# v's tiles between and behind the passes read the passes' own x operands, and VectorE takes the mixes out of PSUM

## The reference

```python
D_MODEL = 1024; SEQ = 2048; DEC_BATCH = 8; DEC_SEQ = 16; PAST_LEN = 128
D_A = D_B = 512; N_GROUPS_A = 4; GMLP_CHUNK = 128; N_HEADS_B = 8; CHUNK = 64; LEFT_CHUNKS = 8
D_IN = 3 * D_A + 4 * D_B

def _project(x, w_in, ln_v_g, ln_v_b):
    h = jnp.einsum('bsd,de->bse', x, w_in)
    u_a = gelu(h[0:512]); v_a = _layernorm(gelu(h[512:1024]), ln_v_g, ln_v_b); z_a = h[1024:1536]
    q, k, v_b, z_b = h[1536:2048], h[2048:2560], h[2560:3072], h[3072:3584]

def _sgu_prompt(u, v, w_s, b_s):                 # chunks of 128 frames, 4 groups of 128 channels
    mix = jnp.einsum('gts,bnsgc->bntgc', jnp.tril(w_s), vc) + b_s.T[None, None, :, :, None]
    return u * mix.reshape(b, s, D_A)

def _band_attn_prompt(q, k, v, rel_table):       # own chunk of 64 and 8 before it, 8 heads
    scores = jnp.einsum('bnqhd,bnkhd->bnhqk', qc, kb) * (HEAD_DIM_B ** -0.5) + bias
    o = jnp.einsum('bnhqk,bnkhd->bnqhd', softmax(where(valid, scores, -inf)), vb)

def _merge(x, a_out, z_a, b_out, z_b, w_out, g, bb):
    y = jnp.concatenate([a_out * jax.nn.silu(z_a), b_out * jax.nn.silu(z_b)], axis=-1)
    return _layernorm(ALPHA * x + jnp.einsum('bse,ed->bsd', y, w_out), g, bb)
```

## Time and profile before

| | |
|---|---|
| median of 3 runs | 1068.24 us |
| the profiled execution, its own time | 1069.9 us |
| its span, first to last instruction | 1068.1 us |
| mean granted TensorE clock | 0.983 |
| PE busy | 1010.1 us, 95% |
| DVE busy | 695.8 us, 65% |
| ACT busy | 526.7 us, 49% |
| POOL busy | 304.6 us, 29% |
| DMA | 158.96 MB, mean 149 GB/s |

### The profile page before, as it was taken

One profiled execution on the slowest core, in us unless ns is written; L12 is line 12 of the kernel. 1 busy time (PEld: TensorE's weight loads), 2 busy tenths in 40 slices (PEclk: granted clock), 3 DMA queues, 4 the chain that ended last, 5 costly groups with the idle time before them and its releaser, 6 DMA issues.

```text
span 1068.1 us, 19316 instructions
## 1 busy us (share of the span) xinstructions
PE 1010.1 (95%) x7460; PEld 866.4 (81%) x7460; DVE 695.8 (65%) x1222; ACT 526.7 (49%) x1035; POOL 304.6 (29%) x269
## 2 busy tenths in 40 slices
PE   8797999999999779999999997999999999999997
PEld 6685877778887669999999986777888888888885
DVE  4453477677576788666555552496777777786665
ACT  4344563344345445333434343575666666666630
POOL 2461334432240744242322200003222222223201
PEclk9898999999999989999999998999999999999999
DMA  8366433336546822323555466585344434433222
GB/s 276 104 200 192 148 99 104 93 89 187 167 141 203 308 79 92 114 75 95 160 175 153 130 217 212 188 278 190 134 147 154 147 133 133 161 115 110 91 80 79
DMA packets 126507, 158.96 MB, mean 149 GB/s; under 512 B 13752, under 2 KB 76368, under 8 KB 126416
## 3 DMA queue, kind: packets, MB, share of 16 engines
q1 hardware_dynamic: 111440, 130.46, 38.1%
q10 hardware_dynamic: 14976, 27.27, 8.5%
HBM read 112.58 MB, written 48.26 MB: 151 GB/s over the span
## 4 chain that ended last, share of the span: by engine, by line
PE 73%; DMA 8%; DVE 7%; issue 3%; POOL 3%; SPq 3%; ACT 2%; ACTq 0%; DVEq 0%; POOLq 0%
PE s_ps L1767 17%; PE oo_ps L1948 15%; PE pt_ps L1767 9%; PE s_ps L1714 8%; PE oo_ps L1910 6%; PE s_ps L1839 5%; PE oo_ps L1767 3%; PE pt_ps L1881 3%; DMA xt_f<-x_tiles 2%; PE pt_ps L1714 2%; PE s_ps L1948 2%; POOL xo_f L925 1%; DMA wp_raw<-w_tok 1%; PE s_ps L1868 1%; PE oo_ps L1735 1%
## 5 line engine op out<-in xcount | busy, mean ns | idle before, releaser
L1767 PE MATMUL s_ps<-xo_h,wf 128*128 128x288 f32 (+1 forms) x960 | 232.6, 326 | 0.9 <-ACT copy L1086 0.9
L1767 PEld LDWEIGHTS s_ps<-xo_h,wf 128*128 128x128 f32 x960 | 163.6, 188 | 13.8 <-DVE xo_l L1361 1.2
L1714 PE MATMUL s_ps<-wp,xt_h 128*128 128x512 f32 x448 | 147.0, 410 | 27.9 <-DVE xt_l L1355 26.8
L1767 PE MATMUL s_ps<-xo_l,wf 128*128 128x288 f32 (+1 forms) x480 | 156.5, 326 | 0.0
L1767 PE MATMUL pt_ps<-xo_h,wf 128*128 128x288 f32 (+1 forms) x480 | 120.5, 328 | 9.0 <-DVE u L1377 7.2
L1714 PEld LDWEIGHTS s_ps<-wp,xt_h 128*128 128x128 f32 x448 | 85.9, 197 | 49.5 <-issue 23.7
L1539 DVE CUSTOM_DVE_ANT_1 prob<-s_ps,bias 128x640 f32<-128x640 f32 (+1 forms) x112 | 85.8, 803 | 59.2 <-PE s_ps L1839 59.0
L1243 ACT ACTIVATE prob<-prob,low 128x640 f32<-128x640 f32 (+3 forms) x128 | 97.4, 762 | 46.5 <-DVE low L1539 46.4
L1355 DVE TENSOR_TENSOR xt_l<-xt_f,xt_h 128x512 fp32r<-128x512 f32 x68 | 63.7, 949 | 82.7 <-ACT xt_h L1057 82.4
L1948 PE MATMUL oo_ps<-wo_h,yh 128*128 128x512 f32 x248 | 100.5, 405 | 0.0
L1349 DVE TENSOR_TENSOR wf<-s,wf 128x512 fp32r<-128x512 f32 x60 | 51.1, 854 | 72.1 <-ACT wf L1052 72.1
(11 more groups left out here) (161 smaller groups left out, 1990.0 us busy)
## 6 DMA issues: line engine op xcount, KB each, us to landing
a<-w_pair ACTq DMA_DIRECT2D x80, 256.0 KB, 2.8
xt_f<-x_tiles SPq DMA_DIRECT2D x68, 256.0 KB, 3.3
r<-x SPq DMA_DIRECT2D x17, 512.0 KB, 3.6
s_k<-st SPq DMA_DIRECT2D x32, 256.0 KB, 2.9
s_q<-st SPq DMA_DIRECT2D x32, 256.0 KB, 2.8
q<-s_q SPq DMA_DIRECT2D x16, 512.0 KB, 4.3
k<-s_k SPq DMA_DIRECT2D x16, 512.0 KB, 5.5
y_out<-r SPq DMA_DIRECT2D x15, 512.0 KB, 2.7
```

The source lines that it names most:

```text
L1714: made = nc.tensor.matmul(out, xx[b][:, kc % HK, :], wp[:, kc, side, :], start=(h, i, a) == (0, 0, 0), stop=(h, i, a) == (1, HK - 1, 2))
L1767: made = nc.tensor.matmul(out, wf[:, p, side, kc, :], xx[pas][p][:, kc, c * n:(c + 1) * n], start=kc == 0 and a == 0 and p in (0, 1, 3, 5) ...
```

## The change

- **v's tiles 0 to 7** take their stationary operand from pass 0's `xo` (`project_half`). Tiles 0 to 3 are operand 0 times the upper half of v's weights and operand 3 times the lower. Tiles 4 to 7 are operand 6 times the lower, operand 1 times the upper, and tile t - 4's product of operand 0, since x's quarter 4 is operand 1 plus operand 0: ScalarE copies that part out (`copy_shared`), VectorE adds it (`add_shared`). Tiles 8 to 11 read operands 0 and 3 of pass 1. Each tile still has 24 matmuls of 512 columns. `xt` is loaded and split for tiles 12 to 16 alone.
- **Pass 1's x** comes in four loads of 1152 KB instead of sixteen of 288 KB, each when its memory is free: operands 4, 0, 6 beside the last pair of pass 0, 3 behind w_freed. Its operands lie in other slots (`X_SLOT`), 1 and 2 share one buffer as sums, and operand 5's sums wait for v's tile 7.
- **The mixes**: VectorE reads them from PSUM, scaled and with the bias row added (`evacuate_mix`, four instructions of 128 columns a tile); `copy_mix` and `scale_mix` are gone. The bias rows are made behind the second tile.
- **Loads**: x for pass 0 is asked for at tiles 1, 4, 7, 10 instead of 0, 1, 3, 5, its sums follow at tiles 3 to 13; the eight writes of `s_skew` go from tile 7 to pass 0, one in each of the first eight pairs; ln_v_g and ln_v_b are loaded at tile 11.

```diff
-X_FIRST = [(kc, p) for kc in range(HK) for p in range(4)]
+X_BEFORE = [[(kc, p) for kc in range(HK) for p in range(4)], [(kc, p) for p in (0, 4, 1, 2) for kc in range(HK)]]
+X_BESIDE = [[(kc, p) for p in (4, 5, 6) for kc in range(HK)], [(kc, p) for p in (3, 5, 6) for kc in range(HK)]]
+X_LOADS = [1, 4, 7, 10]
+X_SLOT = [[0, 1, 2, 3, 4, 5, 6], [4, 0, 3, 6, 2, 1, 5]]
+        v_ps = [tile_ps[0], tile_ps[2], o_ps, out_ps, tile_ps[1], tile_ps[3], o_ps, out_ps]
+        shared = [copies[0], copies[2], copies[1], cs[0]]
 # SP
-                if t == 7:
-                    sp.wait_ge(rel_stored, 32)
-                    for h in range(HEADS):
-                        sp.dma_start(s_skew[h, :, 0:REL], s_rel[h, :].partition_broadcast(P))
+                        if pas == 0 and p == 3 and m < HEADS:
+                            sp.dma_start(s_skew[m, :, 0:REL], s_rel[m, :].partition_broadcast(P))
+                        if m == NP - 1 and p in (3, 5, 6):
+                            sp.wait_ge(proj_done, DONE["f", m, p - 1])
+                            load_xb({3: 4, 5: 0, 6: 6}[p])
 # GpSimd, sum_x of pass 1
+                elif p == 1:
+                    pool.wait_ge(proj_done, DONE["f", NP - 1, 5])
+                    for block_j in (0, 1):
+                        pool.wait_ge(xb_loaded[block_j], 16)
+                elif p == 4:
+                    pool.wait_ge(xb_loaded[3], 16)
+                elif p == 2:
+                    pool.wait_ge(xo_ready, x_pieces(1, kc, 1))
+                else:
+                    pool.wait_ge(proj_done, DONE["v", V_MID - 1])
 # ScalarE
+            def copy_shared(i):
+                act.wait_ge(q_part, i + 1)
+                act.wait_ge(added, 4 * NP)
+                nc.scalar.activation(shared[i][:, 0:512], v_ps[i], ACT.Copy).then_inc(q_copied, 1)
 # VectorE
+            def add_shared(t):
+                dve.wait_ge(proj_done, DONE["v", t])
+                nc.vector.tensor_tensor(st[s][:, 0:512], v_ps[t], shared[t - 4][:, 0:512], ALU.add).then_inc(tile_evac, 1)
+            def evacuate_mix(t):
+                dve.wait_ge(mix_done, t + 1)
+                for g in range(GRP):
+                    made = nc.vector.scalar_tensor_tensor(out=st[s][:, at_g], in0=mix_ps[t % 2][:, at_g], scalar=v_cols[:, g:g + 1],
+                                                          in1=(mix_b if t < PTILES else mix_bs)[:, g, :],
+                                                          op0=ALU.mult, op1=ALU.add)
+                made.then_inc(mix_copied, 1)
-                    if p >= 3:
-                        scale_mix(4 * m + p - 3)
 # TensorE
+                shared_part(0)
+                for i in range(4):
+                    if i < 3:
+                        shared_part(i + 1)
+                    other_part(i)
+                for i in range(4):
+                    project_half(4 + i, 6, 1, True, False)
+                for i in range(4):
+                    project_half(4 + i, 1, 0, False, True).then_inc(proj_done, 1)
...
+                project_half(t, 0, 0, True, False)
+                project_half(t, 3, 1, False, True).then_inc(proj_done, 1)
```

More of the change, by code:

```diff
@@ L218, in xt_place, with xt_loads_before @@
         return 2 + h
[L219 to L227, removed]
+    return 4 + h if kind == "v" and t > V_SPLIT else h
+def xt_loads_before(kind, t):
+    return sum(e[1] % 2 == t % 2 for e in XT_TILES[:XT_TILES.index((kind, t))])
 def xt_user_before(kind, t, h):
-    had = [e for e in TOKEN_TILES if xt_place(*e, h) == xt_place(kind, t, h) and tile_seq(*e) < tile_seq(kind, t)]
+    had = [e for e in XT_TILES[:XT_TILES.index((kind, t))] if xt_place(*e, h) == xt_place(kind, t, h)]
@@ L473, in hybrid_stream_step @@
         w_freed = sem("w_freed")
-        xo_loaded = [[sem(f"xo_loaded{a}_{kc}") for kc in range(HK)] for a in range(PASSES)]
+        xo_loaded = [sem(f"xo_loaded{kc}") for kc in range(HK)]
+        xb_loaded = [sem(f"xb_loaded{j}") for j in range(4)]
         x_summed = sem("x_summed")
@@ new lines, in _ @@
+                    for t in range(V_MID // 2):
+                        store_v(t)
+                    for last in (TILES - 2, TILES - 1):
+                        s, stored = STAGED["va", last][0]
+                        sp.wait_ge(st_stored[s], 16 * (stored + 1 + (last == TILES - 1)))
+                    load_mixb(8)
+                    load_mixb(9)
+                    sp.wait_ge(w_freed, 7 + HK)
+                    load_xb(3)
+                    for t in range(V_MID // 2, V_MID):
+                        store_v(t)
@@ L791, in _ @@
+            for h in range(2):
+                load_xt("v", V_SPLIT + 1, h)
             sp.wait_ge(proj_done, LAST_F)
-            for h in range(2):
-                load_xt("v", V_MID + 2, h)
             for s in range(4):
@@ L990, in _ @@
                 if pas == 0:
-                    for j in range(16):
+                    pool.wait_ge(ya_full, len(ZA_COUNT) // 2)
+                    for j in range(8):
                         sum_x(1, j)
@@ L994, in _ @@
                         sum_w(NP, i)
+                    for j in range(8, 16):
+                        sum_x(1, j)
             pool.wait_ge(proj_done, LAST_F)
@@ L1694, in project_tile @@
             def project_tile(kind, t, h0, h1):
[L1695 to L1696 removed]
+                out = tile_ps[t % 4] if kind == "va" else v_ps[t]
                 if h0 == 0:
@@ L1717, in project_tile @@
                                 made.then_inc(xt_freed, 1)
-                        if last and (h, i) != (1, HK - 1):
+                        if (kind, t) == ("va", TILES - 1) and (h, i) != (1, HK - 1):
                             made.then_inc(w_freed, 1)
```

347 lines of the change are left out of this document (177 added, 170 removed).

## The result

The changed kernel takes 1030.95 us, the median of 4 runs (1029.38 to 1031.89), the kernel before beside it 1067.95 us (4 runs). The ratio is 0.9651, 95% interval [0.9634, 0.9668]: 37 us less. The forecast was 1022 us, its range 1014 to 1036. The profiled execution took 1031.48 us (span 1029.5), 38.4 less than that of before, where the sum had 45.8.

What follows compares the result with a forecast made beforehand. TensorE, busy 95% of the span, was taken as the bound, so only its idle and slow stretches counted; terms 8.7 + 10.2 - 0.3 + 6.6 + 12.6 + 7.0 + 1.0 = 45.8 us gave 1022 us, range 1014 to 1036.

Steps and rivals of the forecast that it cites:

- Bias rows and s_skew's writes: In va's tiles: TensorE's wait for bias rows and the store delayed by eight writes go, gains 8.7 and 10.2 us.
- VectorE takes the mixes: In va's tiles: four PSUM reads a tile take about 1.11 us, fit in 6.34 us, gain or cost 0.
- Rival C: Slower side, va's tiles: GpSimd slows VectorE's mix instructions to 1.78 us each, 4.7 us a tile, total 1088; chance 0.03.
- u's sums: TensorE's waits for u's sums shrink without mix scaling, gain 6.6 us; 0.3 taken for the eight writes in pass 0.
- Between the passes: Pass 0's end to pass 1: gain 16.9 us, less 1.0 for late pieces, 1.3 for a late load or low part.
- rival B: Between the passes: the three 1152 KB loads hold up the pieces of v's weights, total 1028 us; chance 0.08.
- sign for "wrong": Among the signs of a wrong prediction: pass 1 starts over 50 us after pass 0's end.
- signs for "right": Expected traces: no `mix_b` wait, mixes 6.34 us apart, 44 to 47 us between passes, about 2 us wait at product 3.
- Rival A: Between the passes, the sums become the bound and TensorE starts pass 1 about 5 us late, total 1028; chance 0.15.
- Product 3: Pass 1's product 3: a new TensorE wait of 2.0 us, between 0.5 and 4, behind operand 5's sums and `s_104`.
- Behind pass 1: Pass 1's end to the first scores: 34.3 us where five tiles want 27.3, gain 7.0 us.
- The attention: Before the first scores: tile 14's second half is loaded after tile 11 instead of tile 12, gain 1.0 us.

Runs made afterwards that it cites:

- The three edits together: Changed kernel with first shared copy ahead of the pieces' high parts, GpSimd's fourth weight sum ahead of operand 5's sums, operand 6's parts among products 2 to 4: 1023.62 us.
- loads in quarters: Changed kernel with each of pass 1's four 1152 KB x loads issued as four of 288 KB at the same places: 1031.10 us, ratio 0.9637.
- copy first: Changed kernel with ScalarE's first shared copy ahead of the high parts of the last three pieces of v's weights: 1028.15 us, ratio 0.9611.
- operand 6 early: Changed kernel with the high and low parts of pass 1's operand 6 among products 2 to 4 instead of 4 and 5: 1030.38 us, ratio 0.9643.
- both loads held back: Changed kernel with the loads of operands 0 and 6 issued only when the last three pieces of v's weights have landed: 1027.38 us, ratio 0.9611.
- first three edits together: Changed kernel with operands 0 and 6 loaded behind the pieces, GpSimd's fourth weight sum before operand 5's sums, operand 6's parts among products 2 to 4: 1024.72 us.
- `s_104` first: Changed kernel with GpSimd's fourth sum of the weights ahead of operand 5's four sums at pass 1's start: 1030.16 us, ratio 0.9634.

## Why the prediction was right, and what it sized wrong

By the distances in the two profiled executions (the kernel before less the changed one), step by step:

- **Bias rows and s_skew's writes**, forecast 18.9: 138.03 - 118.51 = 19.5. Shown by the traces, and in the trace of each alone. The writes cost nothing to be seen in pass 0.
- **VectorE takes the mixes**, forecast 0: 0 in va. Four instructions take 1.10 to 1.13 us, as `mix_b`'s row said. One of GpSimd's sums beside all four did not slow them, while low parts with two operands in SBUF take 0.76 alone and 1.94 beside GpSimd's sums. By the Trainium skill's rule (SBUF — State Buffer, Who interferes with whom) it should be so, and the trace agrees, though few mixes met a large GpSimd operation. Rival C is refuted.
- **u's sums**, forecast 6.6 less 0.3: pass 0 gave 3.2, and the 3.1 us of pass 1's own waits of u are gone. One wait stays, at pass 0's start: 1.61 us where 0.6 was forecast. With the scaling left out and no mixes on VectorE pass 0 gave 5.2.
- **Between the passes**, forecast 16.9 - 1.0 - 1.3 = 14.6: 60.6 - 50.1 = 10.5. That v's tiles no longer wait for `xt` is read from the two traces; no run has this part of the change alone. Here the step failed that reads "0.5 late", "I take 1.0". Its mechanism (the copy behind the last piece, the pieces slower beside a large load) is what the trace shows, but the piece took 3.5 us more and not 1 to 2, and the term left out that this wait also lowered the clock: 6.8 us at a mean of 0.59 lose 2.8, together 6.5. The 1.3 kept for a late load was not needed; pass 1 starts without a wait. This is rival B, priced right by itself (7 us, less 1.0) and given 0.08: its counter-argument, that the loads are spread by waits on products, did not hold, because operand 0's load was asked for at product 5's start but SP, in order, had a store of z to issue first, and came to it at 315.86, right ahead of the pieces. The prediction's own sign for "wrong", over 50 us from pass 0's end to pass 1, is met by 0.1; of the signs for "right" three were missed with it (44 to 47 us between the passes, 27 to 28 behind pass 1, a clock above 0.99 where the profiled execution had 0.989), and the others came, though sums of other units (`cs`) are still waited for, 1.7 us in all as before. Rival A is not what happened: no sum or low part was waited for there.
- **Product 3**, forecast 2.0: the wait is 2.19, its place and releaser as named; 1.7 more for 3.4 us at a clock of 0.50, not counted.
- **Product 6**, forecast nothing: 1.96, and 1.6 more for 3.4 us at 0.52. The prediction followed the chain of low parts to operand 3 and stopped. It is the second term missed.
- **Behind pass 1**, forecast 7.0: 34.3 - 29.0 = 5.3, as tile 12 waits 1.10 us for a staging copy of ScalarE.
- **The attention**, forecast 1.0: 407.1 - 402.8 = 4.3. Before had waits of 1.36, 1.73, 0.87, 0.68 and 1.21 us in its first 70 us, after 0.43, 0.88 and 0.68. No run tests why more than the first went, so these 3.3 us over the forecast are luck: without them and the 0.6 in va the time would be 1035, at the edge of the range.

The sum of the measured is 19.5 + 3.2 + 10.5 - 4.2 + 5.3 + 4.3 = 38.6, the difference of the spans. Against 45.8 it lacks 4.1 between the passes, some 5.5 at products 3 and 6, 1.7 behind pass 1, and has 3.3 more in the attention and 0.6 in va (0.2 is left over). The largest size that was off is the clock's: three waits of 2 to 3.7 us cost 6.1 us more than their length. The two parts can't be had one by one, though, as the last section shows. The three edits together, which leave one wait of 1.79 us there, end at 1023.62, near the 1022 that was forecast. So the mechanism and the places were right in the main; the sum was 7.2 us too high, and its range was wide enough to hold that.

## What to carry to other kernels

A small transfer on the path was slowed here by a large one on another queue: look at what the other queue holds when the small one is issued, and issue the large one well ahead or, if its own reader can wait, behind it; cutting it up did nothing. An in-order engine that waits for a late transfer holds up everything behind it, so put first what needs no transfer. When you price a new wait, add what a slow stretch behind it may cost (here 0 or 1.7 us behind 2.2 us, 2.8 behind 3.7), and follow the chain one consumer further than the wait you found: the next is often late by what the first one hid.

## What the runs showed of the hardware

- **The same wait lowers the clock or not.** Behind product 3's wait of 2.19 us the granted clock is 0.50 in the changed kernel and 1.00 in the one with loads in quarters, with the same products ahead and behind. It is 0.51 with the copy first and 0.57 with operand 6 early, and 1.00 with the mixes taken twice. At pass 1's start it is 1.00 behind 2.13 us (both loads held back) and 0.60 behind 2.47 (the first three edits together); behind 2.72 between the passes (quarters) it is 1.00, behind 3.6 to 3.9 it fell in all four kernels that had such a wait there. What decides it no run tells. First the changed kernel, then the one with quarters:

```profile
376.60:378.80 2.20, 0.01 (x1) 0.01 (x1) 2.10 (x4) 2.20 (x5) 0.00 (x0) 1.00 0.67 210
379.50:382.90 3.40, 3.40 (x16) 3.40 (x15) 2.00 (x3) 2.81 (x6) 1.15 (x1) 0.50 0.29 105
```

```profile
376.20:378.30 2.10, 0.00 (x0) 0.00 (x0) 2.04 (x4) 2.10 (x5) 0.00 (x0) 1.00 0.69 240
378.40:381.80 3.40, 3.40 (x26) 3.40 (x27) 2.65 (x4) 3.40 (x7) 0.24 (x1) 1.00 0.43 150
```

- **A slow TensorE can hide a slow VectorE.** In the kernel with quarters TensorE runs on at full clock behind product 3. VectorE's two low parts stand beside GpSimd's operations nearly all the time and take 3.68 us where the changed kernel's row above has 2.62, and product 6 waits 4.30 instead of 1.96. It starts 14.1 us behind product 3, in the changed kernel 13.3: the full clock gained nothing, since VectorE set the time. The other kernels agree. Where TensorE kept its clock or had no wait at product 3, product 6 waited 4.21 us (mixes twice), 4.14 (loads behind the pieces) and 3.65 (`s_104` first); where it was slow, 1.99 (copy first). So taking one wait away gave little here: waits and slow stretches traded against each other until all of them were gone.

```profile
388.70 3.68 DVE L1393 TENSOR_TENSOR xo_l<-xo_f,xo_h 128x576 fp32r<-128x576 f32 x2
...
392.44 0.61 PE L1837 MATMUL pt_ps<-xo_h,wf 128*128 128x288 f32 x1 [4.30 <-DVE xo_l L1393]
```
